# MLP gate and up projection: high weights times high and low x in one 512-column product over two PSUM banks

## The reference, cut to what matters

```python
hn = (_rms(x, norm2_g[l]) * (1 + sc2) + sh2).astype(x.dtype)
gate, up = jnp.split(hn @ w_gate_up[l], 2, axis=-1)
x = x + g2 * ((jax.nn.silu(gate) * up) @ w_down[l])
```

## Time and profile before

| what | value |
|---|---|
| median of three runs | 1048.14 us (1047.56 to 1048.99) |
| span of the profiled execution, first to last instruction | 1048.4 us |
| PE busy | 1019.6 us (97%) |
| VectorE (DVE) busy | 752.1 us (72%) |
| ScalarE (ACT) busy | 530.2 us (51%) |
| HBM read | 179.04 MB, 172 GB/s over the span |
| chain that ended last | PE 87%, DVE 7%, ACT 3%, DMA 2% |

### The profile page before, as it was taken

One profiled execution on the slowest core, in us unless ns is written; L12 is line 12 of the kernel. 1 busy time (PEld: TensorE's weight loads), 2 busy tenths in 40 slices (PEclk: granted clock), 3 DMA queues, 4 the chain that ended last, 5 costly groups with the idle time before them and its releaser, 6 DMA issues.

```text
span 1048.4 us, 21565 instructions
## 1 busy us (share of the span) xinstructions
PE 1019.6 (97%) x9120; PEld 897.6 (86%) x9120; DVE 752.1 (72%) x1049; ACT 530.2 (51%) x590; POOL 0.5 (0%) x7
## 2 busy tenths in 40 slices
PE   9999999999999999999999999989999999999998
PEld 7999999999866798989898787659986669999986
DVE  5999957678557668677787866867986775565553
ACT  5674544483353464435555433656687564335331
POOL 0000000000000000000000000000000000000000
PEclk8999999999999999999999999999999999999999
DMA  9454343244326664425343554876352446545441
GB/s 353 162 183 161 129 154 106 97 162 161 123 81 255 236 240 167 150 83 200 122 162 122 178 185 163 320 295 241 123 181 99 161 143 260 218 184 188 157 171 47
DMA packets 26302, 181.47 MB, mean 173 GB/s; under 512 B 3040, under 2 KB 3296, under 8 KB 4960
## 3 DMA queue, kind: packets, MB, share of 16 engines
q1 hardware_dynamic: 25056, 174.66, 45.2%
q10 hardware_dynamic: 1152, 5.45, 1.4%
HBM read 179.04 MB, written 1.05 MB: 172 GB/s over the span
## 4 chain that ended last, share of the span: by engine, by line
PE 87%; DVE 7%; ACT 3%; DMA 2%; issue 1%; SPq 0%; DVEq 0%; ACTq 0%
PE PS L916 84%; DVE WL L1799 2%; DMA RAW<-wst 1%; ACT WH L1386 1%; PE PS L1079 1%; DMA layer<-xt 1%; DVE X L1995 1%; DVE X L1996 1%; PE PS L1157 1%; PE PS L1307 0%; DVE STAT L1977 0%; DVE X L1976 0%; DVE layer_ln L2109 0%; DVE layer L2102 0%; ACT block L1690 0%
## 5 line engine op out<-in xcount | busy, mean ns | idle before, releaser
L916 PE MATMUL PS<-XTH,WH 128*128 128x256 f32 x1392 | 403.7, 290 | 6.2 <-issue 1.5
L916 PE MATMUL PS<-XTL,WH 128*128 128x256 f32 x1392 | 394.8, 284 | 0.0
L916 PE MATMUL PS<-XTH,WL 128*128 128x256 f32 x1392 | 394.7, 284 | 0.0
L1799 DVE TENSOR_TENSOR WL<-RAW,WH 128x2048 fp32r<-128x2048 f32 x138 | 314.2, 2277 | 99.8 <-ACT WH L1386 96.4
L1386 ACT ACTIVATE WH<-RAW 128x2048 fp32r<-128x2048 f32 x138 | 262.7, 1904 | 214.2 <-PE PS L916 208.7
L916 PEld LDWEIGHTS PS<-XTH,WH 128*128 128x128 f32 x1392 | 267.8, 192 | 12.6 <-issue 3.8
L916 PEld LDWEIGHTS PS<-XTL,WH 128*128 128x128 f32 x1392 | 268.0, 193 | 1.6 <-issue 1.4
L916 PEld LDWEIGHTS PS<-XTH,WL 128*128 128x128 f32 x1392 | 267.8, 192 | 0.0
L916 PE MATMUL PS<-WH,YH 128*128 128x512 f32 x224 | 89.6, 400 | 1.1 <-DVE YL L2274 1.1
L916 PE MATMUL PS<-WH,YL 128*128 128x512 f32 x224 | 87.4, 390 | 0.0
L916 PE MATMUL PS<-WL,YH 128*128 128x512 f32 x224 | 87.3, 390 | 0.0
(11 more groups left out here) (293 smaller groups left out, 1112.6 us busy)
## 6 DMA issues: line engine op xcount, KB each, us to landing
RAW<-wst SPq DMA_DIRECT2D x162, 1024.0 KB, 4.9
LNW<-lnrow ACTq DMA_DIRECT2D x3, 1024.0 KB, 6.7
RAW<-wst SPq DMA_DIRECT2D x4, 512.0 KB, 5.7
layer<-xt SPq DMA_DIRECT2D x2, 512.0 KB, 5.3
XR<-x ACTq DMA_DIRECT2D x1, 1024.0 KB, 4.7
out<-X SPq DMA_DIRECT2D x4, 256.0 KB, 3.3
CST<-cst ACTq DMA_DIRECT2D x1, 640.0 KB, 8.7
PT<-pt SPq DMA_DIRECT2D x1, 512.0 KB, 5.6
```

The lines of the kernel that those rows point to most:

```text
L916: return pe.matmul(o, lhsT, rhs, start=start, stop=stop)
L1799: tt(WL[:, i % RAW_RING, 0:n], RAW[:, i % RAW_RING, 0:n], as_float(WH[:, k % SPLIT_RING, 0:n]), ALU.subtract).then_inc(vector_done, 1)
```

## The change

A unit of gate and up now takes two banks, gate in one, up in the other, and four pairs of banks take turns: (4, 5), (6, 7), (0, 1), (2, 3). `XTH` and `XTL` become the two halves of one tile `XT`, at the same addresses, so that one matmul can stream 256 columns of the high part and then 256 of the low part. In each bank, columns 0 to 255 collect high x high and low weight x high x; columns 256 to 511 collect high weight x low x. ScalarE first copies the second halves of both banks to SBUF (step `ffc`), VectorE adds the first halves to them (`ffa`), ScalarE takes silu of the gate part in SBUF (`ff`), and VectorE multiplies, casts and subtracts as before (`ff`). The order lists run the units in ascending j, and the pair of a unit is read to the end by `ffa`.

```diff
+    wide = [(4, 5), (6, 7), (0, 1), (2, 3)]
     for j in range(FF):
-        unit("ff", j, on="TSV", slab=("ff", j), halves=False)
+        step("ff", j, on="TSV", banks=wide[j % 4], slab=(("ff", j),), readers="V", read_in=("ffa", j))
+        step("ffc", j, on="S")
+        step("ffa", j, on="V")
+    while ring[0] != 4:
+        bank()
...
-        XTH = sb("XTH", [P, KC, T], F32R)
-        xtl_at = at[0]
-        XTL = sb("XTL", [P, KC, T], F32R)
+        xtl_at = at[0] + 4 * KC * T
+        XT = sb("XT", [P, 2, KC, T], F32R)
+        XTH, XTL = XT[:, 0], XT[:, 1]
...
-        SG, HT = A3.take(2, T), A3.take(2, T)
+        GU = A3.take(4, T)
...
+            def features_wide(step, ready):
+                split_ready(step.slabs[0])
+                wh, wl = wt(step, KC)
+                for k in range(KC):
+                    if k % 2 == 0:
+                        ready(k // 2)
+                    for a in range(2):
+                        s, o = slice(a * P, (a + 1) * P), PS[:, step.banks[a], :]
+                        mm(o.rearrange("p (x t) -> p x t", x=2), wh[:, k, s], XT[:, :, k, :], start=k == 0, stop=False)
+                        last = mm(o[:, 0:T], wl[:, k, s], XT[:, 0, k, :], start=False, stop=k == KC - 1)
+                return last
...
-                features(step, xt_part(5)).then_inc(tensor_done, 1)
+                features_wide(step, xt_part(5)).then_inc(tensor_done, 1)
...
-            def s_ff(j):
+            def s_ffc(j):
                 act.wait_ge(tensor_done, tensor_at("ff", j))
                 if j >= 2:
                     act.wait_ge(vector_done, vector_at("ff", j - 2))
-                fn(SG[:, j % 2, :], PS[:, bank_of("ff", j), 0:T], ACT.Silu).then_inc(scalar_done, 1)
+                b = bank_of("ff", j)
+                fn(GU[:, j % 2 * 2:j % 2 * 2 + 2, :], PS[:, b:b + 2, T:2 * T], ACT.Copy).then_inc(scalar_done, 1)
+
+            def s_ff(j):
+                act.wait_ge(vector_done, vector_at("ffa", j))
+                g = GU[:, j % 2 * 2, :]
+                fn(g, g, ACT.Silu).then_inc(scalar_done, 1)
...
+            def v_ffa(j):
+                dve.wait_ge(scalar_done, scalar_at("ffc", j))
+                b, both = bank_of("ff", j), GU[:, j % 2 * 2:j % 2 * 2 + 2, :]
+                tt(both, both, PS[:, b:b + 2, 0:T], ALU.add).then_inc(vector_done, 1)
+
             def v_ff(j):
                 dve.wait_ge(scalar_done, scalar_at("ff", j))
-                link(tt(HT[:, j % 2, :], SG[:, j % 2, :], PS[:, bank_of("ff", j), T:2 * T], ALU.mult))
+                g, u = GU[:, j % 2 * 2, :], GU[:, j % 2 * 2 + 1, :]
+                link(tt(u, g, u, ALU.mult))
                 h, l = y_tile(j)
-                link(dve.tensor_copy(h, HT[:, j % 2, :]))
-                tt(l, HT[:, j % 2, :], as_float(h), ALU.subtract).then_inc(vector_done, 1)
+                link(dve.tensor_copy(h, u))
+                tt(l, u, as_float(h), ALU.subtract).then_inc(vector_done, 1)
```

More of the change, by code:

```diff
@@ L512 @@
 first:out2:0:1 first:out2:1:1 out2:0:1 out2:1:1 ada:10:0 ada:10:1 ada:11:0 adat:10 xt:5:0 xt:5:1 xt:5:2 xt:5:3
-ada:11:1 ff:0 adat:11 ff:1 ff:2 ff:3 ff:5 ff:4 ff:6 ff:8 ff:7 ff:9 ff:11 ff:10 ff:12 ff:13 ff:14 ff:15 ff:16 ff:17
-ff:18 ff:19 ff:21 ff:20 down:0:0 down:0:1 down:0:2 down:0:3 down:0:4 first:down:0:5 down:1:0 down:0:5 down:1:1
-down:1:2 down:1:3 down:1:4 first:down:1:5 down:1:5
+ada:11:1 ff:0 adat:11 ff:1 ff:2 ff:3 ff:4 ff:5 ff:6 ff:7 ff:8 ff:9 ff:10 ff:11 ff:12 ff:13 ff:14 ff:15 ff:16 ff:17 ff:18 ff:19
+ff:20 ff:21 down:0:0 down:0:1 down:0:2 down:0:3 down:0:4 first:down:0:5 down:1:0 down:0:5 down:1:1 down:1:2 down:1:3
+down:1:4 first:down:1:5 down:1:5
 """
@@ L543 @@
 pv:15 rms:1:0:0 split:105:128 rms:1:0:1 split:106:130 rms:1:1:0 rma:1 rmt:1:0 rms:1:1:1 rmt:1:1 ada:10:1 xt:5:0 xt:5:1
[L544 to L549, removed]
+xt:5:2 xt:5:3 split:107:133 ada:11:1 ffc:0 split:108:134 ff:0 ffc:1 split:109:135 ff:1 ffc:2 split:110:136 ff:2 ffc:3
+split:111:137 ff:3 ffc:4 split:112:138 ff:4 ffc:5 split:113:139 ff:5 ffc:6 split:114:140 ff:6 ffc:7 split:115:141 ff:7
+ffc:8 split:116:142 ff:8 ffc:9 split:117:143 ff:9 ffc:10 split:118:144 ff:10 ffc:11 split:119:145 ff:11 ffc:12
+split:120:146 ff:12 ffc:13 split:121:147 ff:13 ffc:14 split:122:148 ff:14 ffc:15 split:123:149 ff:15 ffc:16
+split:124:150 ff:16 ffc:17 split:125:151 ff:17 ffc:18 split:126:152 ff:18 ffc:19 split:127:153 ff:19 ffc:20
+split:128:154 ff:20 ffc:21 split:129:155 ff:21 split:130:156 split:131:157 split:132:158 split:133:159 split:134:160
+split:135:161 split:136:162 split:137:163 split:138:164
 """
@@ L584 @@
 split:105:128 out2:0:1 out2:1:1 rmsb:1:0 rmsb:1:1 adat:10 xt:5:1 xtl:5:0 xt:5:3 xtl:5:1 xtl:5:2 xtl:5:3 split:106:130
[L585 to L590, removed]
+adat:11 split:107:133 ffa:0 split:108:134 ff:0 ffa:1 split:109:135 ff:1 ffa:2 split:110:136 ff:2 ffa:3 split:111:137
+ff:3 ffa:4 split:112:138 ff:4 ffa:5 split:113:139 ff:5 ffa:6 split:114:140 ff:6 ffa:7 split:115:141 ff:7 ffa:8
+split:116:142 ff:8 ffa:9 split:117:143 ff:9 ffa:10 split:118:144 ff:10 ffa:11 split:119:145 ff:11 ffa:12 split:120:146
+ff:12 ffa:13 split:121:147 ff:13 ffa:14 split:122:148 ff:14 ffa:15 split:123:149 ff:15 ffa:16 split:124:150 ff:16
+ffa:17 split:125:151 ff:17 ffa:18 split:126:152 ff:18 ffa:19 split:127:153 ff:19 ffa:20 split:128:154 ff:20 ffa:21
+split:129:155 ff:21 split:130:156 split:131:157 split:132:158 split:133:159 first:down:0:5 split:134:160 down:0:5
+split:135:161 split:136:162 split:137:163 split:138:164 first:down:1:5 down:1:5
 """
@@ L1725, in _ @@
                      "hr": s_hr, "rms": s_rms, "rma": s_rma, "rmt": s_rmt, "feat": s_feat, "qn": s_qn, "ga": s_ga, "gb": s_gb, "val": s_val,
-                     "gm": s_gm, "score": s_score, "turn": s_turn, "pv": s_pv, "mln": s_mln, "ff": s_ff}
+                     "gm": s_gm, "score": s_score, "turn": s_turn, "pv": s_pv, "mln": s_mln, "ffc": s_ffc, "ff": s_ff}
             mine, table = 0, None
@@ L2308, in _ @@
                      "feat": v_feat, "qn": v_qn, "mb": v_mb, "mlz": v_mlz, "xtl": v_xtl, "score": v_score, "ratio": v_ratio, "mln": v_mln,
-                     "out2": v_out2, "down": v_down, "ff": v_ff}
+                     "out2": v_out2, "down": v_down, "ffa": v_ffa, "ff": v_ff}
             dve.wait_ge(gpsimd_done, gpsimd_at("setup"))
```

## The result

| | before | changed |
|---|---|---|
| median, 12 runs each | 1049.97 us | 1054.68 us |
| lowest and highest | 1047.56, 1051.87 | 1051.1, 1056.74 |
| ratio, with its 95% interval | | 1.0047 (1.0035 to 1.0059) |
| span of the profiled execution | 1048.4 us | 1054.3 us |

What follows compares the result with a forecast made beforehand. The prediction took TensorE's own rate to bound the MLP. Its terms, -4.7 + 4.6 - 0.2 + 1.1 = +0.8, plus 2.0 for the clock, gave +2.8 on 1048.1, so 1050.9 us, range 1048.4 to 1052.8.

Steps and rivals of the forecast that it cites:

- Part 1: Gate and up on TensorE: two matmuls replace three per weight tile, 347 ns for 360, saving 4.7 us over 352.
- the prediction's own sign of being wrong: Stated in advance for the PE timeline: the forecast is wrong if a wide product keeps more than 230 ns.
- Part 2: First unit: TensorE waits for ScalarE's copy of `MROW` out of bank 5; 4.6 us later, 0.2 us coming back.
- Part 3: Second unit: TensorE waits for VectorE to read bank 7, held by `adat:11`; costs 1.1 us.
- Parts 4 and 5: ScalarE's and VectorE's new steps, the unit order and slab loads: all hidden by slack, no cost.
- Part 6: TensorE idle 5 us ahead of the first unit: clock falls from 2.4 to 1.2 GHz, costing 2.0 us.
- my one and two stretches: Clock price: one half-clock stretch of 3.4 us over dense matmuls costs 1.7 us, two cost 3.4 us.
- The sum: Whole kernel: -4.7 + 4.6 - 0.2 + 1.1 = +0.8 us, plus 2.0 for the clock, +2.8 us.
- The clock didn't stay: Rival: TensorE's clock stays up after the idle stretch ahead of the first unit; 1048.9 us, chance 0.20.
- the wait was there: Rival: no wait at `ff:0`, as the `MROW` copy is done by then; 1044.5 us, chance 0.05.
- neither chain became the bound: Rival: VectorE's or ScalarE's chain becomes the bound in the units; up to 15 us, 1066, chance 0.03.
- The rival on the two-run read: Rival: the wide product's read in two runs of 256 columns costs 10 ns or more; 1054.4 us, chance 0.07.

Runs made afterwards that it cites:

- e5_busy5: The changed kernel with five products of the ones matrix filling TensorE's wait ahead of unit 0; ratio to before 1.0019.
- e7_again: The changed kernel, unedited, profiled a second time; 1052.8 us, one run.
- e2_busy: The changed kernel with eleven products of the ones matrix, 9.1 us in all, ahead of unit 0's wait; ratio to before 1.0063.
- e1_banks: The changed kernel with banks dealt anew so that neither unit 0 nor unit 1 waits for its bank; ratio to before 0.9962, median 1045.58 us.
- e6_three: e1_banks with three narrow products in place of each wide and narrow pair, all else kept; ratio to before 1.0002.
- e4_contig: e1_banks with the wide product reading 512 columns in one run, which sums other products; ratio to before 0.9964.
- e10_unit1: e1_banks with unit 1 on banks 6 and 7 again, so that it alone waits; ratio to before 0.9978.
- e11_banks_again: e1_banks, unedited, run once more for a second profile; 1045.3 us.
- e8_again: The changed kernel, unedited, profiled a third time; 1053.01 us, one run.
- e3_before_wait: The kernel before, with only the banks of units 0 and 1 swapped so that unit 0 waits for its bank; ratio to before 1.0059.

## Why the prediction was right or wrong

- **Part 1, fewer matmuls: the step that failed.** The sum took 227 + 120 = 347 ns for a pair, 352 x 13.3 = 4.7 us. The pair has a second pace of 353 ns, which leaves 352 x 6.7 = 2.3 us of gain, and three of the five profiles with the change's own banks had it (the two of the changed kernel at 1056.31 and 1053.01 us, and `e5_busy5`; `e7_again` and `e2_busy` did not). Why it comes is open. That the 347 came out at the fast pace was in part luck: the prediction has each product keep its own distance, but the wide one kept 232 ns and the narrow one 115 (means of the starts of units 3 to 20 in `e1_banks`), and 236 and 117 at the slow pace (changed kernel). So the prediction's own sign of being wrong, a wide product above 230 ns, was there.
- **What Part 1 had overlooked.** Narrow products kept 120 ns throughout gate and up, and mixed neighbours were judged by four single rows. For wide products the trace of before did hold a second pace, in `down`. The nine read for 227 ns take their stationary operand (the one that a weight load puts in place) from `YH` and `YL`. The products of the last six of the 22 tiles, which lie in `EH` and `EL`, start 233 ns apart, for instance fifteen of them in 3.49 us:

```profile
1005.36 0.40 PE L916 MATMUL PS<-WH,EH 128*128 128x512 f32 x1
...
1008.85 0.40 PE L916 MATMUL PS<-WH,EH 128*128 128x512 f32 x1
```

This pace sets in with no wait ahead of it, and at the same products in the changed kernel. Six ns more on each of 352 wide products would have been 2.1 us in the sum. Whether it has the same cause as the 353 ns of the pairs, no run shows.
- **The gain of Part 1, and its weight load.** The gain itself is shown: 4.6 us (`e6_three` against `e1_banks`). The removed weight load gave back no more than its 13 ns, so the rule on loads that the prediction quotes (the Trainium skill, TensorE: Matmul & The Clock Gate, Part 3, "The mechanism") is spoken against by the runs as well. The same section of the Trainium skill also names a load into a background weight buffer as one that is pulled ahead, and that part the runs don't contradict. The two-run read is free (`e4_contig`).
- **Part 2, unit 0's bank: right.** Idle 4.99 us against 0.35, released by ScalarE's copy, 4.6 us as worked out. (The engine needed 0.09 us behind the copy, not the 0.05 that the prediction put in.)
- **Part 3, unit 1's bank: right.** 1.1 us worked out, 1.2 measured alone (`e10_unit1` against `e1_banks`; against `e11_banks_again`, whose unit 0 had the slow pace too, 1.1).
- **Parts 4 and 5, cover by other engines and the loads: right.** `e6_three` puts all of it at -0.1 us in the MLP. The 3.4 us of VectorE a unit was low, since the stretch of the earlier trace rows reaches 19 us into `down`; from 874.5 to 983 us alone it is 3.5.
- **Part 6, the clock: right in kind, and 2.0 against 2.3 us in size.** The half-clock stretch over work was 4.8 us, between my one and two stretches.
- **The sum.** In `e7_again`, where the pace was the fast one, the MLP is 191.47 - 188.56 = +2.9 us, which is the forecast's +2.8. In the profile shown first it is 193.82 - 188.56 = +5.3, and in `e8_again` +5.5, the extra being the pace. The +4.9 of the twelve runs, by the ratio, lies nearer to the slow ones; how many of the twelve had the slow pace is not known, since one has a profile.
- **The level.** 1050.9 was built on a median of three at 1048.14; on the later one of 1049.97 the same sum gives 1052.8, at the edge of the range, and the measured 1054.68 is still 1.9 above it. I gave the range no room for the level's own shift, although three runs spread by 1.4 us.
- **The rivals.** The clock didn't stay, the wait was there, and neither chain became the bound. The rival on the two-run read foresaw a dearer wide product by 10 ns and 1054.4 us. That this is close to the 1054.68 measured is a coincidence: a pair was dearer by 6.6 ns at the slow pace, and reading in one run gained nothing (`e4_contig`).

## What to carry to other kernels

When a step gets more buffers of a ring (here PSUM banks), list who held each of them last and what stands in front of that holder's reader: two bank numbers cost 5.7 us of waiting and 2.3 of clock, more than the edit could gain. The 5 us wait of TensorE here cost its length and then half-speed work behind it, in each of four profiles; deal the buffers so that such a wait goes, or fill it. Measure a small gain in a version without the new waits before it is given up: the same products on other banks made the kernel 0.38% faster. And when a sum multiplies one distance by hundreds of products, read that distance in every group of the trace that has the width, not in one.

## What the runs showed of the hardware that was not expected

- A stream of alternating 512- and 256-column products runs at one of two steady paces, 347 or 353 ns a pair, in the same program. The change from one to the other was seen behind a wait (`e5_busy5`, 347 to 353) and at a product of another kind without a wait (`e11_banks_again`, 353 to 347). What picks it is open; no run controlled it.
- Products of 512 columns alone have two paces as well, 227 and 233 ns; here the place is the same in the kernel before and in the changed one, and goes with the tile that the stationary operand comes from (`YH` and `YL`, or `EH` and `EL`).
- Narrow products alone kept 120 ns in the units of the three profiles that have them, also once the clock was back up (`e3_before_wait`); at half clock they started 0.21 us apart.
- Five products of the ones matrix, 4.3 us in all, in a wait of 5 us, held the clock at 2.4 GHz (granted clock 1.00); with the wait empty it fell in each of the four profiles that had it (the changed kernel three times, `e3_before_wait`).
- A product of the float32 ones matrix with 512 columns took 0.85 us, against 0.23 for an fp32r product of that width.
